# First attention's far value tiles computed already turned, merged scalings and adds in two down projections, and two reordered seams

## The reference, cut to what matters

```python
DIL_CONFIGS = ((128, 1), (512, 4), (2048, 16))
for g, (window, dil) in enumerate(DIL_CONFIGS):
    o, l = _dilated_group(qkv[:, :, g, 0], qkv[:, :, g, 1], qkv[:, :, g, 2], window, dil, slopes[g])
wts = jax.nn.softmax(jnp.stack(lses), axis=0)
o = jnp.sum(wts[..., None] * jnp.stack(outs), axis=0)
...
h = h + rmsnorm(mix, g[1])
ff = conv_ffn(rmsnorm(h, g[2]), ffn_w_up[l], ffn_conv[l], ffn_w_down[l])
h = h + rmsnorm(ff, g[3])
```

## Time and profile before

| | |
|---|---|
| median of 3 runs | 3410.52 us (3409.12 to 3412.01) |
| profiled execution | 3411.94 us, of which the span from first to last instruction is 3410.1 |
| TensorE busy | 3367.1 us, 99% |
| VectorE, ScalarE, GpSimd busy | 74%, 51%, 4% |
| mean granted clock of TensorE | 0.997 |
| instructions | 65717 |

### The profile page before, as it was taken

One profiled execution on the slowest core, in us unless ns is written; L12 is line 12 of the kernel. 1 busy time (PEld: TensorE's weight loads), 2 busy tenths in 40 slices (PEclk: granted clock), 3 DMA queues, 4 the chain that ended last, 5 costly groups with the idle time before them and its releaser, 6 DMA issues. The chain is left out here.

```text
span 3410.1 us, 65717 instructions
## 1 busy us (share of the span) xinstructions
PE 3367.1 (99%) x25107; PEld 3146.1 (92%) x25107; DVE 2521.6 (74%) x3720; ACT 1726.3 (51%) x2640; POOL 136.2 (4%) x130
## 2 busy tenths in 40 slices
PE   9999999999999999999999999999999999999998
PEld 8998899989998989898899889999999998799987
DVE  6886888887888778787888865557785367777863
ACT  4563655545554545454545545446555344555552
POOL 0100202000200100000001000000000000000000
PEclk9999999999999999999999999999999999999999
DMA  4333223332333322222233321211223321123332
GB/s 141 111 102 113 88 88 104 111 111 94 99 105 111 107 75 87 75 87 87 69 106 106 116 93 63 75 62 64 99 98 99 94 75 43 39 75 100 98 99 81
DMA packets 89676, 311.33 MB, mean 91 GB/s; under 512 B 10816, under 2 KB 15296, under 8 KB 89472
## 3 DMA queue, kind: packets, MB, share of 16 engines
q1 hardware_dynamic: 89056, 307.19, 27.7%
q0 software_dynamic: 416, 1.29, 0.1%
HBM read 306.34 MB, written 2.10 MB: 90 GB/s over the span
## 5 line engine op out<-in xcount | busy, mean ns | idle before, releaser
L872 PE MATMUL ps<-x_hi,w_hi 128*128 128x264 f32 (+2 forms) x1840 | 572.8, 311 | 2.6 <-ACT pair L2844 0.9
L872 PE MATMUL ps<-x_hi,w_lo 128*128 128x264 f32 (+2 forms) x1840 | 562.9, 306 | 0.0
L872 PE MATMUL ps<-x_lo,w_hi 128*128 128x264 f32 (+2 forms) x1840 | 561.9, 305 | 0.0
L872 PE MATMUL ps<-h_hi,w_hi 128*128 128x264 f32 (+3 forms) x1282 | 406.7, 317 | 4.3 <-DVE h_lo L3160 1.9
L872 PE MATMUL ps<-h_hi,w_lo 128*128 128x264 f32 (+3 forms) x1282 | 395.9, 309 | 0.0
L872 PE MATMUL ps<-h_lo,w_hi 128*128 128x264 f32 (+3 forms) x1282 | 395.1, 308 | 0.0
L872 PEld LDWEIGHTS ps<-x_hi,w_hi 128*128 128x128 f32 x1840 | 347.1, 189 | 32.0 <-issue 10.2
L872 PEld LDWEIGHTS ps<-x_hi,w_lo 128*128 128x128 f32 x1840 | 347.8, 189 | 14.7
L872 PEld LDWEIGHTS ps<-x_lo,w_hi 128*128 128x128 f32 x1840 | 346.3, 188 | 15.8
L2953 DVE TENSOR_TENSOR w_lo<-raw,w_hi 128x1024 fp32r<-128x1024 f32 x214 | 260.9, 1231 | 109.8 <-ACT w_hi L1808 105.8
L967 PE MATMUL ps<-t_hi,w_hi 128*128 128x256 f32 x1152 | 322.7, 280 | 0.0
(11 more groups left out here) (417 smaller groups left out, 8829.0 us busy)
## 6 DMA issues: line engine op xcount, KB each, us to landing
raw<-wstream SPq DMA_DIRECT2D x577, 512.0 KB, 3.3
res<-xT SPq DMA_DIRECT2D x8, 256.0 KB, 7.4
out<-res SPq DMA_DIRECT2D x8, 256.0 KB, 2.2
near_bias<-consts POOLq DMA_DIRECT2D x1, 512.0 KB, 3.9
g_chunk<-consts POOLq DMA_DIRECT2D x1, 264.0 KB, 3.1
g_keep<-consts POOLq DMA_DIRECT2D x1, 256.0 KB, 3.2
par<-params SPq DMA_DIRECT2D x1, 232.5 KB, 7.3
far_bias<-consts POOLq DMA_DIRECT2D x1, 128.0 KB, 2.6
```

The source lines that it names most:

```text
L872: m = pe.matmul(ps[:, bank, 0:n], w[:, slot, wt, :], x[:, k, c0:c0 + n], start=first and q == 0, stop=last and q == 2)
```

## The change

Seven of the eight passes of the first attention (`p` from 1) get `value_rows`: for the two far groups together, x is the stationary operand, 128 tokens of one residue (every fourth token), and the weights of units 7 and 8 move past, 256 columns. So the result has tokens on its partitions and needs no transposes. Four residues, each 8 blocks x 3 products: 96 matmuls. It starts when both units' low parts are there, and counts both units as done at its end. ScalarE's `store_rows` takes each residue out of PSUM.

TensorE:

```diff
+        def turned(p):
+
+            return 3 + 4 * (p - 1) if p else 0
+
+        def value_slots(st, p):
+
+            a, b = attend_slot(st, p, 7), attend_slot(st, p, 8)
+            return slice(a, b + 1) if a < b else slice(b, a + 1, a - b)
+
+        def value_place(st, p, g):
+
+            return 3 - g if g and p and attend_slot(st, p, 7) > attend_slot(st, p, 8) else g
...
+                        pe.wait_ge(s_evac, st["t0"] + 9 * p + 9)
...
                         for g in (1, 2):
                             for r in range(R4):
-                                both(lambda out: out[:, r * P:(r + 1) * P], lambda half: val[:, r, g, head(half)],
+                                both(lambda out: out[:, r * P:(r + 1) * P], lambda half: val[:, r, value_place(st, p, g), head(half)],
                                      lambda half: scored[:, half, g - 1, r * P:(r + 1) * P], (g, r) == (1, 0), False)
...
                     if t == 3:
                         turn_maxima(p)
-                        turn_values(p, 2)
+                        if not p:
+                            turn_values(p, 2)
...
+                def value_rows(p):
+
+                    t, slots = st["t0"] + 9 * p, value_slots(st, p)
+                    pe.wait_ge(s_lo, st["u0"] + 9 * p + 9)
+                    for r in range(R4):
+                        if r < 2:
+                            pe.wait_ge(s_evac, t + 6 + r)
+                        else:
+                            pe.wait_ge(A["val"], 3 * p + 1 if r == 2 else 3 * p + 3)
+                        for k in range(KD):
+                            hi, lo = (x[:, k, META:T].rearrange("p (i r) -> p r i", r=R4)[:, r, :] for x in x_src)
+                            for n, (x, w) in enumerate(((hi, w_hi), (hi, w_lo), (lo, w_hi))):
+                                m = pe.matmul(ps[:, r % 2, 0:2 * P], x, w[:, slots, k, :],
+                                              start=k == 0 and n == 0, stop=k == KD - 1 and n == 2)
+                            if k == KD - 1:
+                                if r < R4 - 1:
+                                    m.then_inc(A["vtr"], 1)
+                                else:
+                                    m.then_inc(s_unit, 2)
+                            if (r, k) == (0, 5):
+                                turn_values(p, 0)
+                                scores(p, 2)
+                                scores(p, 3)
...
                     for g in range(3):
                         pack1(p, g)
-                    for j in range(6, 9):
-                        unit_of(p, j)
+                    unit_of(p, 6)
+                    value_rows(p)
```

ScalarE:

```diff
-                        if v >= 2:
+                        if p >= 2:
+                            act.wait_ge(A["vtr"], turned(p - 1) + 1)
+                        elif v >= 2:
                             act.wait_ge(A["vtr"], v - 1)
...
 
                 def store(p, g):
-                    v = 3 * p + g
-                    act.wait_ge(A["vtr"], v + 1)
+                    act.wait_ge(A["vtr"], turned(p) + g + 1)
                     if p >= 1:
                         act.wait_ge(A["pv"], p)
                     act.activation(val[:, :, g, :], ps[:, 6 + g % 2, :].rearrange("p (i n) -> p i n", i=R4), ACT.Copy)\
...
+                def store_rows(p, r):
+
+                    if r < R4 - 1:
+                        act.wait_ge(A["vtr"], turned(p) + r + 2)
+                    else:
+                        act.wait_ge(s_unit, st["u0"] + 9 * p + 9)
+                    act.wait_ge(A["pv"], p)
+                    act.activation(val[:, r, 1:3, :], ps[:, r % 2, 0:2 * P].rearrange("p (g n) -> p g n", g=2), ACT.Copy)\
+                        .then_inc(A["val"] if r < 2 else s_evac, 1)
 
...
+                    snap(p, 0, 1)
                     high(p, 0, 3)
-                    snap(p, 0, 1)
                     high(p, 1, 0)
                     snap(p, 0, 3)
-                    store(p - 1, 2)
+                    if p == 1:
+                        store(0, 2)
                     snap(p, 0, 4)
...
                         high(p + 1, 0, 1)
+                        store_rows(p, 0)
                         store(p, 0)
-                        take(p, 7)
+                        for r in range(1, R4):
+                            store_rows(p, r)
                         high(p + 1, 0, 2)
-                        store(p, 1)
-                        take(p, 8)
...
                     take(p, 6)
                     split(nxt + 1, (nxt + 1) % RING)
-                    store(p, 0)
                     for k in range(3, 6):
                         att_high(k)
-                    take(p, 7)
+                    store_rows(p, 0)
+                    store(p, 0)
+                    store_rows(p, 1)
                     att_high(6)
-                    store(p, 1)
-                    take(p, 8)
-                store(KD - 1, 2)
+                    store_rows(p, 2)
+                    store_rows(p, 3)
```

```diff
-                    act.activation(dst, src, ACT.Copy).then_inc(s_za if h == 0 else s_evac, 1)
+                    act.activation(dst, src, ACT.Copy, scale=par_of(st["after"], k) if merged(st) else 1.0)\
+                        .then_inc(s_evac if h is None or h == parts(st) - 1 else s_za, 1)
...
                 def late_tile(q):
                     act.wait_ge(s_unit, st["u0"] + len(chunks) * (full + q + 1))
-                    take(full + q, 1, full + m + q)
+                    take(full + q, parts(st) - 1, full + (parts(st) - 1) * m + q)
...
                 if m == 1:
-                    squares((0,))
                     lead(1)
-                    squares((1, 2, 3))
+                    squares(range(4))
+                    lead(2)
+                    squares(range(4, KD))
                     late_tile(0)
-                    squares(range(4, KD))
-                    lead(2)
...
                 roots(tok, (0, s_sqp, st["s0"] + KD, 2, s_root2, 4 * st["i0"]))
+                for k in range(4):
+                    high(st, 0, k)
                 if m == 1:
                     roots(tok, other)
-                    for k in range(KD):
+                    for k in range(4, KD):
                         high(st, 0, k)
                 else:
-                    for k in range(4):
-                        high(st, 0, k)
```

VectorE:

```diff
+                def scaled(h, k0, k1):
+
+                    c, n = part_cols(st, h), part_of(st, h)[1]
+                    dve.wait_ge(s_root1, 4 * st["v0"] + 2 * h + 2)
+                    r = rstd[:, c].rearrange("p (a n) -> p a n", a=1).to_broadcast([P, k1 - k0, n])
+                    dve.tensor_tensor(mix[:, k0:k1, c], mix[:, k0:k1, c], r, ALU.mult).then_inc(s_mx, k1 - k0)
+
+                def added(h, k0, k1):
+
+                    c = part_cols(st, h)
+                    dve.wait_ge(s_mx, st["a0"] + KD * h + k1)
+                    dve.tensor_tensor(res[:, k0:k1, c], res[:, k0:k1, c], mix[:, k0:k1, c], ALU.add)\
+                        .then_inc(s_final if final(st) else s_add, k1 - k0)
+
+                if final(st):
+                    half = KD // 2
+                    scaled(0, 0, half)
+                    if parts(st) == 3:
+                        add_square(1, full + 1)
+                    scaled(0, half, KD)
+                    added(0, 0, half)
+                    added(0, half, KD)
...
+                    for k0, k1 in ((0, 4), (4, 8)) if parts(st) == 3 else ((0, 4), (4, 6), (6, 8)):
+                        scaled(parts(st) - 1, k0, k1)
+                        added(parts(st) - 1, k0, k1)
+                    return
...
+                def second_half():
+                    if merged(st):
+                        by_half(1)
+                        return
...
+                def by_half(h):
+                    for k0 in (0, KD // 2):
+                        scaled(h, k0, k0 + KD // 2)
+                        added(h, k0, k0 + KD // 2)
+
                 if m == 1:
-                    for k in added_on_vector(st):
-                        add(0, k, s_addv)
-                    late_tile(0)
+                    by_half(0)
                     lead(1)
                     lead(2)
+                    late_tile(0)
```

```diff
+            def run_idle(n):
+
+                pe.wait_ge(s_idle, 1)
+                for _ in range(n):
+                    pe.matmul(ps[:, 7, 0:2 * P], idle[:, 0:P], idle[:, :], start=True, stop=True)
...
+            run_idle(IDLE)
...
             def load(st):
+                load_silu()
                 split(0, 0)
-                load_silu()
...
                     late_tile(0)
-                    lead(1)
...
-                    sums_of(st, 1)
+                    if follower(st)["kind"] == "renorm":
+                        squares_of(follower(st), 0, range(SQUARES))
+                    sums_of(st, parts(st) - 1)
...
             def renorm(st):
-                squares_of(st, 0, range(KD))
```

(83 more changed lines are left out.)

58 lines of the change are left out of this document (26 added, 32 removed).

## The result

| | before | after |
|---|---|---|
| median of the runs | 3410.55 us (3409.12 to 3412.01, 4 runs) | 3479.07 us (3477.74 to 3481.35, 4 runs) |
| profiled execution, its span | 3411.94, 3410.1 | 3477.74, 3475.8 |
| matmuls in the trace | 25107 | 25399 |
| mean granted clock of TensorE | 0.997 | 0.999 |

After takes 1.020 times as long as before (95% interval 1.0188 to 1.0212). I forecast 3403.9 us; the time lies 75 us above it and 69 above the end of my range. What came true is the rival *strided loads*, 16 us above its own upper bound of 3463.

What follows compares the result with a forecast made beforehand. TensorE, with a matmul in flight 99% of the time, was taken as the bound. Terms -4.4 + 0.6 - 1.1 - 1.9 + 0.4 = -6.4 us gave 3404.1 on the median, stated as 3403.9, range 3399 to 3410 us.

Steps and rivals of the forecast that it cites:

- strided loads: Rival, first attention: weight loads of every fourth token are slower and set the matmul pace, 3443 to 3463 us; chance 0.16.
- the first term: Far value tiles, first attention: cheaper matmuls without transposes gain 0.63 us a pass, 4.4 in seven, if loads run as now.
- The slack: Weight loads under 256-column matmuls: a load takes 0.112 us, leaving some 8 ns to spare; 120 ns under 512 columns.
- value rows, load as now: First attention's far value tiles: 4.4 us gained in seven passes (2.7 to 5.2) if new loads run as present ones.
- waits at the pass border: Between attention passes: later weight blocks just fit before TensorE's widening; 0.1 us a pass allowed, 0.6 lost (0 to 1.5).
- the step of 16 bytes: Stationary x at every fourth token: load taken at the lower end, 0.112 us, no extra cost; upper bounds 40 or 59 us.
- first merged stage: Second block's first feed-forward down projection: merged scalings and adds bring the next first product 1.1 us sooner (0.5 to 1.5).
- the end: Kernel's very end: merged scalings and adds after the second root finish 1.9 us sooner (1.5 to 2.1).
- renorm: Reordered renorm seam: TensorE restarts 1.0 us sooner, but that returns as a wait; 0.4 us lost (-1.0 to +2.0).
- start: Kernel start: six idle matmuls and an earlier ScalarE table load, while memory loads still bind; 0 (0 to -0.5).
- all but the attention: Terms outside the attention: first merged stage -1.1, the end -1.9, renorm +0.4, start 0 us.
- the third rival: Renorm pays too: 1.0 us gained in place of 0.4 lost, start gives 0.5; 3402 us, inside the forecast, no separate chance.

Runs made afterwards that it cites:

- experiment 6: Kernel after, but stationary x is 128 tokens in a row and each value-row matmul streams 64 columns instead of 256: 3435.75 us.
- experiment 7: Kernel after, but stationary x is 128 tokens in a row and each value-row matmul has 32 moving columns: 3435.13 us.
- experiment 12: Before plus the attention part alone, with 128 tokens in a row as stationary operand: 3405.98 us against 3411.53, ratio 0.9983.
- experiment 1: Kernel after, but stationary x is 128 tokens in a row instead of every fourth: 3401.55 us against 3410.64 for before, ratio 0.9973.
- experiment 4: Kernel after without its attention part (merged stages, renorm, start and idle matmuls kept): 3406.92 us against 3410.64 for before, ratio 0.9989.
- experiment 5: Kernel after, strided x kept, but each of the 96 value-row matmuls streams 64 columns instead of 256: 3499.95 us.

## Why the prediction was wrong

**The step that failed** stands behind the first term: "I take the lower end", 0.112 us for a load of x at every fourth token, with a chance of 0.16 for the other case. The load costs 0.235 to 0.237, so the term that I put at nothing is 77.5 us. My bracket was wrong, too: its upper end of 0.207, from ScalarE's strided write, lies below the measured load. The writes of another engine did not bound this read.

I argued that the moving side reads 512 columns in 0.2356 us, 0.46 ns an element, and a load asks for one in 0.875. That divides by the wrong thing. Those 512 columns lie in a row, and fill 128 lines of 16 bytes: 1.84 ns a line. Measured loads are 128 lines in 0.235 to 0.237 us (1.84 to 1.85), 96 in 0.176 to 0.178 (1.83 to 1.85), and 64, which would take 0.118, in 0.121 where the stream alone takes 0.119. The same row, read by lines, would have given 0.236 for the new load, and 3403.9 + 672 x (0.236 - 0.1195) = 3482 us. That the moving side is itself held by lines no run here shows; the two paces may agree by chance. TensorE's clock alone does not set it either: 256 columns take 0.118 us at full clock and 0.213 at half (experiment 6), 1.8 times as long and not twice.

The Trainium skill, Advanced Engine Details and Errata, Memory Cachelines, asks for two hits on a 16-byte line for full speed. The runs agree, with 0.121 us at two hits, 0.178 at one and a third, 0.237 at one. I had cited it against the change, and still let the indirect row outweigh it.

**The slack** was read rightly: 0.112 there, 0.111 bare in experiment 7. (Two of the six loads read there belong to matmuls of 128 columns, L1582; the four of L1584 alone give 0.45/4 = 0.112 too.) I had written that the rival decides from a load of 0.129 us. With so little room and 672 bare loads, the chance of 0.16 was too small. That the mechanism stood among my rivals does not make the forecast right: I named it and weighed it wrongly.

**The other terms**, in us:

| term | forecast | measured | from |
|---|---|---|---|
| value rows, load as now | -4.4 | -5.5 to -5.8 | experiment 12 |
| waits at the pass border | +0.6 | 0 | widening's row, no wait |
| the step of 16 bytes | 0 | +77.5 | after less experiment 1 |
| first merged stage | -1.1 | -0.7 | landmarks |
| the end | -1.9 | -1.75 | landmarks |
| renorm | +0.4 | -0.4 | landmarks |
| start | 0 | not told from 0 | landmarks of 11 kernels |
| all but the attention | -2.6 | -3.7 | experiment 4 |

The sum without the step is 3401.55 us in experiment 1, where I had 3403.9. The value rows lie just beyond my end of -5.2, which was worked out with 0.118 for each matmul of 256 columns; of the 1.2 us beyond -4.4 the transposes of experiment 12 are 0.6. At the first merged stage the second half gave part of the gain back. The renorm's gain is the third rival's, at less than its size. The start: idle matmuls do not bring the data sooner, TensorE still waits at 8.72 (1.53 us); its stretch at half clock ends at 12.5 us and not at 14.0, by the distances from start to start, and then it waits for a low part at 14.34. Apart from the start, the terms that are read from landmarks come from one pair of executions; experiment 4 holds their sum, and no run isolates one of them.

## What to carry to other kernels

Before an operand becomes the stationary one, count the 16-byte lines that 128 of its columns touch, times 1.85 ns and at least 0.111 us, and set that against the stream that covers it: four-byte elements in a row or two apart fit under 256 columns, three apart only under some 390 (0.178 us at 0.46 ns a column, an estimate), four apart under 512. Where a stream covers its loads by only 8 ns, "about the same" is no price for a new kind of load. And where a bracket rests on writes or on another engine, widen it on both sides, and divide a memory's pace by lines as well as by elements before it is used as a counter-argument.

## What the runs showed of the hardware that I had not expected

- A strided load's pace does not follow TensorE's clock: 0.235 to 0.237 us at a granted clock of 1.00 and of 0.50, where a load in a row goes from 0.111 to 0.213 us.
- Fewer columns made the kernel slower. In experiment 6 TensorE ran matmuls of 64 columns from 1324.97, at 0.111 us and in flight all the time; about 1329.3 the granted clock fell to 0.50 and stayed there beyond the end of the value rows, into the next pass's products (0.213 us for 256 columns). The whole took 3435.75 where 256 columns took 3401.55: 34 us more. From 1250 to 1660 the mean granted clock was 0.90, which is 82 us at half: 41 us lost, less the 5 that the shorter distances save. Experiment 7 repeats it (3435.13), and in experiment 5 it fell near 1338. With 256 columns at the same strided pace, in after, it stayed at 1.00. TensorE's busy share is 1.00 in the windows of all of them, so it does not announce this; what makes the clock fall no run here isolates.
